# Feed-forward tiles: wide and narrow matmuls alternating by input block, in place of eight wide and then eight narrow

## The reference

```python
D_MODEL, SEQ, DEPTH, D_FF = 1024, 256, 2, 2816

def swiglu(h, w_in, w_out):
    a, b = jnp.split(h @ w_in, 2, axis=-1)
    return (jax.nn.silu(a) * b) @ w_out

for l in range(DEPTH):
    h = rms_norm(x, ffn1_norm_pre[l])
    x = x + 0.5 * rms_norm(swiglu(h, ffn1_w_in[l], ffn1_w_out[l]), ffn1_norm_post[l])
    h = rms_norm(x, mix_norm_pre[l])
    y = token_mixer(h, mem, ...)
    x = x + rms_norm(y, mix_norm_post[l])
    h = rms_norm(x, ffn2_norm_pre[l])
    ...                      # swiglu again, with ffn2_w_in and ffn2_w_out
```

## Time and profile before

| | |
|---|---|
| median of 3 runs | 1771.53 us (1769.86 to 1772.73) |
| profiled execution | 1767.01 us |
| its span, first to last instruction | 1765.2 us |
| mean granted clock of TensorE in it | 0.997 |
| TensorE busy (matmuls) | 1721.0 us, 97% |
| VectorE busy | 1244.2 us, 70% |
| ScalarE busy | 954.3 us, 54% |
| DMA | 311.65 MB, mean 177 GB/s |

### The profile page before, as it was taken

The page is one execution under the profiler, slowest core; times in us unless marked ns, Lnnn a source line. Parts: engine busy times, 40 slices in busy tenths (PEclk is TensorE's granted clock), DMA queues, the critical chain, the costliest instruction groups (busy, mean ns, idle before and its releaser), DMA issues. The chain is left out here.

```text
span 1765.2 us, 28382 instructions
## 1 busy us (share of the span) xinstructions
PE 1721.0 (97%) x10506; PEld 1480.9 (84%) x10506; DVE 1244.2 (70%) x2347; ACT 954.3 (54%) x1622; POOL 18.7 (1%) x20
## 2 busy tenths in 40 slices
PE   7999999999999999999999999999999999999998
PEld 6888889998878888888799988788878878768887
DVE  6666577567876667666577678766677896885775
ACT  5444454566555446444545565544556556563474
POOL 1000000000000000000000000000000000000000
PEclk9999999999999999999999999999999999999999
DMA  8445554534445554454556535455554544203531
GB/s 312 187 181 199 190 191 179 227 144 180 180 181 200 190 212 157 183 203 185 190 183 230 201 117 212 157 204 183 198 188 150 205 150 179 103 6 143 199 123 60
DMA packets 29905, 311.65 MB, mean 177 GB/s; under 512 B 3312, under 2 KB 3696, under 8 KB 4848
## 3 DMA queue, kind: packets, MB, share of 16 engines
q1 hardware_dynamic: 28944, 307.18, 46.4%
q0 software_dynamic: 864, 3.15, 0.6%
HBM read 309.26 MB, written 1.05 MB: 176 GB/s over the span
## 5 line engine op out<-in xcount | busy, mean ns | idle before, releaser
L491 ACT ACTIVATE region_r<-ring 128x1024 fp32r<-128x1024 f32 x495 | 514.9, 1054 | 356.2 <-PE psum L884 335.2
L497 DVE TENSOR_TENSOR ring_r<-ring,region_r 128x1024 fp32r<-128x1024 f32 x487 | 581.3, 1220 | 132.5 <-ACT region_r L491 127.0
L884 PE MATMUL psum<-xs_r,region_r 128*128 128x256 f32 (+2 forms) x3160 | 580.5, 331 | 2.4 <-ACT region_r L491 1.3
L884 PEld LDWEIGHTS psum<-xs_r,region_r 128*128 128x128 f32 (+1 forms) x3160 | 466.2, 188 | 65.3 <-issue 8.7
L884 PE MATMUL psum<-xs_r,ring_r 128*128 128x256 f32 x2344 | 316.5, 277 | 0.0
L884 PEld LDWEIGHTS psum<-xs_r,ring_r 128*128 128x128 f32 x2344 | 302.9, 188 | 15.8
L884 PE MATMUL psum<-region_r 128*128 128x512 f32 (+2 forms) x960 | 304.3, 383 | 0.0
L884 PE MATMUL psum<-region_r,xs_r 128*128 128x512 f32 (+2 forms) x1056 | 272.0, 351 | 6.5 <-DVE region L2697 3.0
L884 PEld LDWEIGHTS psum<-region_r,xs_r 128*128 128x128 f32 x1056 | 183.5, 189 | 36.6 <-ACT xs_r L1808 4.5
L884 PEld LDWEIGHTS psum<-region_r 128*128 128x128 f32 (+2 forms) x960 | 175.9, 185 | 33.0
L884 PE MATMUL psum<-ring_r,region_r 128*128 128x512 f32 (+1 forms) x440 | 156.9, 374 | 0.0
(11 more groups left out here) (255 smaller groups left out, 1599.8 us busy)
## 6 DMA issues: line engine op xcount, KB each, us to landing
ring<-in_weights SPq DMA_DIRECT2D x192, 1536.0 KB, 6.2
gpost<-in_posts POOLq DMA_DIRECT2D x6, 512.0 KB, 5.1
cst<-in_const SPq DMA_DIRECT2D x1, 1213.0 KB, 22.8
xs<-in_mem SPq DMA_DIRECT2D x1, 1024.0 KB, 5.7
x<-in_x SPq DMA_DIRECT2D x1, 1024.0 KB, 8.1
out<-x SPq DMA_DIRECT2D x2, 512.0 KB, 2.6
pars<-in_par SPq DMA_DIRECT2D x1, 368.0 KB, 6.2
p<-in_par SPq DMA_DIRECT2D x1, 206.0 KB, 22.8
```

Of the source, the lines that this page charges most:

```text
L491: eng.activation(unit.high, unit.raw, ACT.Copy).then_inc(h_ready, 1)
L497: eng.tensor_tensor(unit.low, unit.raw, unit.high.bitcast(F32), ALU.subtract).then_inc(l_ready, 1)
L884: ins = pe.matmul(bank, lhsT, rhs, start=start, stop=stop)
```

## The change

In `wide_tile` the two loops over the eight input blocks become one. For each block the wide matmul with the high weights is followed at once by the narrow one with the low weights. The wait for the low part of the unit stands before the first matmul, beside the wait for the high part. The first wide still starts the accumulation in the bank, and the last narrow still ends it and raises `full`. Nothing else differs: the same sixteen matmuls with the same operands, the same units, buffers and signals.

```diff
                 unit = Split(u, it)
                 to = job.bank.rearrange("p (c t) -> p c t", c=2 * NT)
                 pe.wait_ge(h_ready, unit.count)
+                pe.wait_ge(l_ready, unit.count)
                 for kk in range(KD):
                     mm(to, unit.high[:, kk * P:(kk + 1) * P], h_both[:, :, kk, :], kk == 0, False)
-                pe.wait_ge(l_ready, unit.count)
-                for kk in range(KD):
                     mm(to[:, NT:2 * NT, :], unit.low[:, kk * P:(kk + 1) * P], hH[:, :, kk, :], False, kk == KD - 1,
                        signal if kk == KD - 1 else None)
```

## The result

| | before | after |
|---|---|---|
| median of 7 runs | 1771.53 us (1767.82 to 1773.41) | 1779.73 us (1776.20 to 1782.92) |
| profiled execution | 1767.01 us | 1782.92 us |
| its span | 1765.2 us | 1781.1 us |
| mean granted clock in it | 0.997 | 0.994 |
| one step (gate, value, down tile) | 8.293 us | 8.400 us |

The ratio after to before is 1.005, with a 95% interval of 1.0037 to 1.0063: the change costs 6.6 to 11.2 us. The forecast was no change (1770.6 us), with a range from 1766.5 to 1777.5.

What follows compares the result with a forecast made beforehand. TensorE's matmul queue was taken to bound the feed-forwards. Reordering at -1.4 us plus the earlier wait at +0.5 us gave -0.9 us, so 1770.6 us, with a range from 1766.5 to 1777.5 us.

Steps and rivals of the forecast that it cites:

- The bound: In full feed-forward steps TensorE is busy throughout, so its queue of matmuls sets the time; a step takes 8.293 us.
- (a), the order: Alternating wide and narrow in 168 feed-forward tiles: -17 ns per two tiles, -1.4 us in all.
- the discount: In gate and value tiles, a wide behind a narrow takes 388 ns, about 6 ns cheaper than behind a wide.
- its surcharge of 6 ns: In gate and value tiles, a narrow behind a wide is 5 to 7 ns dearer than behind a narrow; taken as 282 ns.
- the second rival: Each switch of width costs in feed-forward tiles, the discount perhaps paid back by the next matmul: +8.0 us, 1779.5 us; chance 0.13.
- the value tile's sum: Value tile's 5372 ns lie within 12 ns of steady 5360, taken to show its change of width and back costs nothing.
- The bound from above: Upper limit for (a), the order, in gate and value tiles: wides stay at 394 ns, narrows pay 283; +7.5 us.
- both its marks: Signs for the second rival: a wide of 398 after the value tile's 388; narrows of 279, 277 after the gate tile's 283.
- Durations for spacings: For TensorE matmuls, a duration 10 ns longer was taken to put off the next matmul by 10 ns.
- (b), the wait: Earlier low-part wait idles TensorE only before the first value tile of layer 0's second feed-forward: +0.5 us.
- The loads: In tiles, weight loads run one matmul ahead; a narrow takes 114 ns, the streaming rate, with no load surcharge to hide.
- The third wait: Rival: three waits instead of two at each tile's head cost 0.09 us in 168 tiles, +15 us, 1786 us; chance 0.05.

Runs made afterwards that it cites:

- lone_narrows: Each tile reordered to wide wide narrow three times, then two wides and five narrows, against the kernel before; step 8.293 us, 1772.16 us (one run).
- lone_wides: Each tile reordered to five wides, narrow narrow wide three times, then two narrows, against the kernel before; step 8.320 us, 1769.64 us (one run).
- wait_first: Kernel before with only the low-part wait moved before the first wide; 1773.34 us against 1770.74, ratio 1.0008, step 8.293 us.
- shift 0: Inputs' buffer begins at a whole line of 128 columns, not 16 columns off; steps 8.307 us (eight wides, eight narrows) and 8.387 us (alternating).
- eights: The order of the kernel before, eight wides then eight narrows in a tile; step 8.293 us with the inputs' buffer in its old place.
- the other three places: Inputs' buffer 0, 64 or 32 columns off the weights' grid instead of 16, old order; 1783.22, 1784.26 and 1784.38 us, one run each.

## Why the prediction was wrong

**The bound.** Right. The feed-forward is TensorE's from end to end, and what a matmul costs beside its neighbour set the result.

**(a), the order: the step that failed.** It was to be -1.4 us and is +9.0. The prediction took "388 for such a wide and 282 for such a narrow". The narrow was right (281). The wide is at 397, not 388, fifteen in a step that were to have the discount. In spacings it is 234.2 ns where the discount gives 225.0 and the steady wide 233.3, beside a narrow of 119.1 where the steady one has 113.3: so the narrow keeps its surcharge of 6 ns and no wide pays for it. The 388 came from one wide in each value tile, the only place of the feed-forwards with a wide behind a narrow, and there it stands behind eight narrows and in front of another wide. Groups of two show the same 388 behind two narrows and in front of a wide, and in `lone_narrows` a wide gets 225.0 ns even behind a single narrow, when a second wide follows. With wides in twos the step stays at 8.293; a single wide behind two narrows (`lone_wides`) has 225 ns four times of six, and the two narrows behind it give back more than that. The discount was in part a loan, as the second rival said: the wide behind it takes 398 (235.7 ns). My reason against that rival, that the value tile's sum is within 12 ns of steady, was true, and misread: it shows that one change of width costs nothing, in runs of eight, and says nothing of runs of one.

**The bound from above** was nearly right for the two tiles as a sum, with the parts dealt out otherwise: wides at 394 and narrows at 283 were to add 89 ns a step, wides at 397 and narrows at 281 added 91. What it left out is the down tile, whose first wides come behind the new order: 2.751 in place of 2.735 us, 16 of the 107 ns. With the wait it makes 9.2 to 9.5 where the rival gave 8.0. The rival's time, 1779.5 us, is within 0.3 us of the measured median, closer than its parts deserve, so that is in part luck; it had a chance of 0.13, and that was the error: both its marks, 398 behind 388 and the tail 279, 277 behind 283, stood in the rows.

**Durations for spacings.** The prediction let a duration 10 ns longer put off the next matmul by 10. That holds only to 2 or 3 ns, which is the size of the terms here: a wide of 388 goes at 225.0 ns, one of 389 at 226.7, one of 394 at 233.3, one of 397 at 234.2. The starts of the loads give the spacing directly.

**(b), the wait.** Right in place and size: 0.51 us in the changed kernel and 0.53 by itself, forecast 0.5. The margins of 0.56 to 11 us elsewhere held.

**The loads.** That a narrow has no load surcharge to hide behind a wide agrees with the result: narrows of the changed kernel's feed-forwards did not fall below 279. The Trainium skill, "TensorE: Matmul & The Clock Gate", section "Back-to-back issue gap", makes the spacing of a load and multiply stream depend on both; a gain by pairing them did not appear in any of nine alternating kernels.

**The third wait** is excluded: `wait_first` has it and keeps the step at 8.293 us.

**What stays open.** That the price depends on the order and on the address is shown. What in the chip makes it is not. Nor do order and address settle every spacing: outside these steps the same run of narrows goes at 113.3 or at 117.8 ns, as shown above, so something else counts too; how such a run begins may be it, which was not tried. The steady spacings are 113.3, 226.7 and 233.3 ns, and all step times found (8.293, 8.307, 8.320, 8.347, 8.353, 8.387, 8.400, 10.207) are 6.7 ns, or a multiple of it, apart within rounding. So over a whole step TensorE seems to lose or keep units of 6.7 ns, while single spacings (225.0, 235.7, 119.3) don't keep to them; that is a reading of the numbers, not a test. Other places than the four, and moving the weights' buffers instead, were not tried.

## What to carry to other kernels

A spacing read at the seam of two long runs is no price for a pattern made of seams: look at the matmul after the cheap one, and sum over the whole cycle that the new order would repeat. When matmuls of two widths must be mixed, keep at least two wides together; runs of two, four and eight cost the same at this place of the buffers (twos and fours were tried at no other), and a single wide between narrows cost up to 6.7 ns, 0.5% of the kernel. Judge such edits by the length of a repeated step in the trace, which resolves a nanosecond where the kernel's time varies by microseconds. But where an edit reaches beyond the step, look at the rest too: with shift 0 and eights the step is 13 ns longer, 1.1 us in all, and the kernel some 9 us.

## What the runs showed of the hardware

- The durations of the same matmul in the same order change with where its moving operand lies in SBUF against the weights: 394 and 276 ns at 16 columns, 389 and 283 at 0, with the step the same at 0 and 64. Across the kernel, with its mixers and tail, the other three places cost some 9 to 11 us (1783.22, 1784.26 and 1784.38 us with eights, against 1773.99, 1773.99 and 1773.11, one run each). Of this the feed-forwards have 1.1 us at shifts 0 and 64 and 4.6 at 32, by the traces; the rest is in mixers and tail, where at shift 0 the 62 matmuls shown above go at 283 (120.0 ns) in place of 276 (113.3).
- The same run of 256-column matmuls, at the same addresses and a granted clock of 1.00, went at 113.3 ns in one execution and at 117.8 in another (276 and 281 in the rows of the tail, kernel before and changed kernel).
- The Trainium skill, "TensorE: Matmul & The Clock Gate", section "Back-to-back issue gap", gives N / 2.4 + 2.5 ns for a warm matmul taken by itself, which makes 215.8 at 512 columns and 109.2 at 256, and says that a stream of loads and multiplies goes faster than this at 512. The trace does not agree: in this format, at a granted clock of 1.00, with a load at every matmul, the steady spacings are 226.7 or 233.3 ns at 512 columns and 113.3 to 120 at 256. The measurement decides.
- Four pieces of 128 columns as moving operand cost the same as 512 in a row (8.293 us a step in both).
